# One maximum and one reciprocal for both heads of a pair, in four attention stages of a fused two-block network

## The chip, the cores and the metric

The program runs on one core of a Trainium2 chip. The metric is the device time of one execution in microseconds. Several executions of a kernel are timed; the median stands for it.

## The reference, cut to what matters

The network has two blocks over 512 tokens of width 1024. It holds many matrix products (projections, MLPs, a convolution, a Fourier mixer) and seven kinds of attention, all with 64 wide values and this softmax:

```
s = jnp.where(mask, s.astype(jnp.float32), -jnp.inf)
m = jnp.max(s, axis=-1, keepdims=True)
p = jnp.exp(s - m)
return p / jnp.maximum(jnp.sum(p, axis=-1, keepdims=True), 1e-30)
```

In the neighbourhood attention of the second block a bias is added to the scores of the 256 near keys before the maximum: `s_nb = s_nb + bias[None]`. Everything is float32.

## The kernel before, in words

The program is a list of stages; each of the five engines walks the list and waits on semaphores. Four stages are attention. In each the work is cut into **pairs**: 128 queries (a query tile) of two heads, g = 0 and 1. The pairs of the four stages are:

- the first (from about 226 to 306 us of the profile): 16 causal pairs, in groups of four with 128, 256, 384 and 512 keys, then 16 pairs of a sliding window with 128 or 256 keys and a sink column;
- the second (600 to 755 us): 16 causal pairs as above, whose scores have a second, rotated part, then four rounds of 4 pairs with 31 keys and 8 causal pairs (two groups of four);
- the third (975 to 1175 us): 32 pairs with 768 keys (the "wide" code: the scores of the two heads fill three PSUM banks), then 16 pairs with 256 keys;
- the fourth (2104 to 2232 us): 32 pairs with 512 keys, 256 near ones with the bias and 256 of the context.

The order of work is written out by hand for each engine; `i` counts pairs.

- **TensorE (PE)** at step i: `scores(i)` (lines 1915 to 1939), which first waits until the exponentials of pair i-2 have read the same banks; then `turn(i-2)` (L1953), which transposes the probabilities of pair i-2 into PSUM in up to two "turns", over two banks that alternate; then a part of `weigh` (L1976), the product with the values, for a chunk of two earlier pairs.
- **VectorE (DVE)** at step i: `negmax(i)`, the negated maximum of head 0 and of head 1 (L2918; in the fourth stage each has an addition of the bias ahead, L2914, and waits for it); then `scale(i-1)`, a reciprocal (L2927) and a multiplication of the probabilities (L2933, with gates L2930) for each head; then some copies of turned tiles (L2944) and, after a head pair's last chunk, `take` (L2953, L2957, L2963).
- **ScalarE (ACT)** at step i: the exponential of head 0 and of head 1 (L2335, each followed by a read of its accumulated sum), then the copies of turned tiles of pair i-2 from PSUM (L2347); in the wide stage the copies come first.

The maxima, sums and reciprocals are columns of one small tile. The exponential of head g waited for the maximum of head g alone where a head has at most 512 keys, and for both maxima where it has more:

```
act.wait_ge(negmax_ready, 2 * pair["id"] + 2 if nk > BANK else u + 1)
```

A turn of pair i-2 can start when three things are there: its probabilities are scaled, the bank's last contents have been copied away by ScalarE, and TensorE has come to it.

Of the kernel before, what the change touches and what calls it, by code (L numbers as in the profile page):

```python
# [17 lines left out]
ALU = mybir.AluOpType  # L18
ACT = mybir.ActivationFunctionType
AX = mybir.AxisListType.X  # L20
# [6 lines left out]
ST = S // P  # L27
# [6 lines left out]
BANK = 512  # L34
# [6 lines left out]
ROWS = S // GRID  # L41
# [4 lines left out]
STRIP = 8  # L46
NA_COLS, NA_KEYS = 32, 256
# [217 lines left out]
def build_program(nc, dram, out_dram, stages_kept=10000):  # L265
    ctx = ExitStack()
    with ctx:
# [3 lines left out]
        def sem(name):  # L271
            return ctx.enter_context(nc.semaphore(name))
# [24 lines left out]
        small = sb("small", [P, 64])  # L297
# [7 lines left out]
        psum = ctx.enter_context(nc.psum_tensor("psum", [P, 8 * BANK], F32))  # L305
# [36 lines left out]
        scores_ready, negmax_ready, probs_ready = sem("scores_ready"), sem("negmax_ready"), sem("probs_ready")  # L342
        exp_done, turned = sem("exp_done"), sem("turned")
# [551 lines left out]
        for t in range(4):  # L895
# [6 lines left out]
                gate=lambda qt, g, c=3 * t: GC[:, qt, 12 * g + c:12 * g + c + 1]))  # L902
            for br, (kk, v0) in enumerate(((KS, 0), (KW, 128))):
# [4 lines left out]
                    gate=lambda qt, g, c=3 * t + br + 1: GC[:, qt, 12 * g + c:12 * g + c + 1]))  # L908
# [328 lines left out]
        for t in range(8):  # L1237
# [4 lines left out]
                bias=lambda qt, g, t=t: bias_buf[t % 2][:, g, qt].rearrange("p (r g c) -> p g r c", r=ROWS, c=STRIP),  # L1242
# [766 lines left out]
        def _(act):  # L2009
            steps = [0]  # L2010
            n = dict(tile=0, sq=0, mean=0, unit=0, read=0, scaled=0, idx=0, misc_pe=0, misc_act=0, norm=0, pv=0, normed=0,
                     ctx=0, conv=0, ada=0)
# [288 lines left out]
            def bias_copy(_, i):  # L2301
# [5 lines left out]
                if c == BIAS_STEPS - 1:  # L2307
                    act.wait_ge(bias_copied, i + 1)
                    for h in range(8):
# [7 lines left out]
                        bias=bias_copy, shift=nothing, masked=nothing, compress=compress, compressed=compressed, csquare=context_square,  # L2317
                        csum=context_root, cnorm=context_shift, modrows=lambda *_: copy_rows(), modturn=nothing)

            def attention(st):  # L2320

                pairs = st["pairs"]

                def exponential(pair, i, g):

                    p, nk, off = pair["p"], pair["nk"], pair["off"][g]
                    u = 2 * pair["id"] + g
                    c = u % 8

                    act.wait_ge(negmax_ready, 2 * pair["id"] + 2 if nk > BANK else u + 1)  # L2330
                    if i >= 2:
                        before = [t["seq"] for t in pairs[i - 2]["turns"] if g in t["gs"]]
                        act.wait_ge(turned, before[-1])
                    more = pair["sink"] is not None
                    nc.scalar.activation(pair["probs"][g][:, 0:nk + more], psum[:, off:off + nk + more], ACT.Exp,  # L2335
                                         bias=small[:, c:c + 1], accum_out=small[:, 8 + c:9 + c]).then_inc(exp_done, 1)

                def copies(pair, i):

                    for t in pair["turns"]:  # L2340
                        if t["who"] != "act":
                            continue
                        dst, src = turned_views(pair, t)
                        act.wait_ge(turned, t["seq"])
                        if i >= 4:
                            act.wait_ge(pv_done, st["chunks"][i // 2]["seq"] - 2)
                        nc.scalar.activation(dst, src, ACT.Copy).then_inc(act_copied, 1)  # L2347

                for i in range(len(pairs) + 2):
                    if st["wide"] and i >= 2:  # L2350
                        copies(pairs[i - 2], i - 2)
                    if i < len(pairs):
                        exponential(pairs[i], i, 0)
                        exponential(pairs[i], i, 1)
                    if not st["wide"] and i >= 2:
                        copies(pairs[i - 2], i - 2)
                act.wait_ge(act_copied, pairs[-1]["copied"][0])
# [29 lines left out]
        def _(dve):  # L2387
# [3 lines left out]
            def step(ins):  # L2391
                ins.then_inc(dve_steps, 1)
                steps[0] += 1

            def settle():
                dve.wait_ge(dve_steps, steps[0])

            def chain(ins):

                step(ins)  # L2400
                settle()
# [498 lines left out]
            def attention(st):  # L2900

                pairs, chunks = st["pairs"], st["chunks"]

                def negmax(pair, g):

                    p, nk, off = pair["p"], pair["nk"], pair["off"][g]
                    u = 2 * pair["id"] + g
                    c = u % 8
                    dve.wait_ge(scores_ready, pair["id"] + 1)
                    if p["bias"] is not None:  # L2910
                        if pair["qt"] == 0 and g == 0:
                            dve.wait_ge(bias_in[pair["pi"] % 2], 16 * BIAS_LOADS * (pair["pi"] // 2 + 1))
                        near = psum[:, off:off + NA_KEYS].rearrange("p (g r c) -> p g r c", r=ROWS, c=STRIP)
                        chain(nc.vector.tensor_tensor(near, near, p["bias"](pair["qt"], g), ALU.add))  # L2914
                        if pair["qt"] == ST - 1 and g == 1:
                            dve.sem_inc(bias_used, 1)
                    nk += pair["sink"] is not None
                    nc.vector.tensor_reduce(small[:, c:c + 1], psum[:, off:off + nk], AX, ALU.max,  # L2918
                                            negate=True).then_inc(negmax_ready, 1)

                def scale(pair, g):

                    p, nk = pair["p"], pair["nk"]
                    u = 2 * pair["id"] + g
                    c = u % 8
                    dve.wait_ge(exp_done, u + 1)
                    chain(nc.vector.reciprocal(small[:, 24 + c:25 + c], small[:, 8 + c:9 + c]))  # L2927
                    pb, by = pair["probs"][g][:, 0:nk], small[:, 24 + c:25 + c]
                    if p["gate"] is not None:
                        nc.vector.tensor_scalar(pb, pb, by, p["gate"](pair["qt"], g), ALU.mult,  # L2930
                                                ALU.mult).then_inc(probs_ready, 1)
                    else:
                        nc.vector.tensor_scalar(pb, pb, by, None, ALU.mult).then_inc(probs_ready, 1)  # L2933

                def copies(pair, i):

                    for t in pair["turns"]:
                        if t["who"] != "dve":
                            continue
                        dst, src = turned_views(pair, t)  # L2940
                        dve.wait_ge(turned, t["seq"])
                        if i >= 4:
                            dve.wait_ge(pv_done, chunks[i // 2]["seq"] - 2)
                        nc.vector.tensor_copy(dst, src).then_inc(dve_copied, 1)  # L2944

                def take(chunk):

                    if not chunk["takes"]:
                        return
                    p, c0 = chunk["p"], chunk["c0"]  # L2950
                    dve.wait_ge(pv_done, chunk["seq"])
                    if st["wide"]:
                        nc.vector.tensor_copy(p["dst"][:, c0:c0 + CHUNK], bank(chunk["bank"], CHUNK)).then_inc(o_taken, 1)  # L2953
                        return
                    src = bank(chunk["bank"], p["n"])
                    if p["z"] is not None:
                        nc.vector.tensor_tensor(p["dst"][:, 0:p["n"]], src, p["z"][:, 0:p["n"]],  # L2957
                                                ALU.mult).then_inc(o_taken, 1)
                    else:
                        dst = p["dst"][:, 0:p["n"]]  # L2960
                        if p["runs"] is not None:
                            dst, src = rows_of(dst), by_rows(src)
                        nc.vector.tensor_copy(dst, src).then_inc(o_taken, 1)  # L2963

                for i in range(len(pairs) + 8):
                    if i < len(pairs):
                        negmax(pairs[i], 0)
                        negmax(pairs[i], 1)
                    if 0 <= i - 1 < len(pairs):
                        scale(pairs[i - 1], 0)  # L2970
                        scale(pairs[i - 1], 1)
                    if 0 <= i - 2 < len(pairs):
                        copies(pairs[i - 2], i - 2)
                    j = i - (5 if st["wide"] else 6)
                    if j >= 0 and j % 2 == 0 and j // 2 < len(chunks):
                        take(chunks[j // 2])
                dve.wait_ge(o_taken, chunks[-1]["taken"])
# [244 lines left out]
```

## Time and profile before

| | us |
|---|---|
| median of 3 executions | 3860.42 |
| lowest, highest | 3854.82, 3867.68 |
| span of the profiled execution | 3863.2 |
| TensorE busy | 3731.4 |
| VectorE busy | 1986.4 |
| ScalarE busy | 968.1 |
| GpSimd busy | 585.1 |

The profiled execution is one of its own; the page gives its span and no other time, and its span is 2.8 us above the median. TensorE is busy for 97% of the span, but matmuls are pipelined and "busy" is not "at its peak". In a row of the timeline the first number is the start, the second the duration, and the bracket at the end is how long the engine had been idle and what released it.

### The profile page before, as it was taken

How to read it: one execution, taken by the hardware profiler on the slowest of the kernel's cores; microseconds unless marked ns; L12 is line 12 of the kernel's file. 1: busy time of each engine (PE TensorE's matmuls, PEld its weight loads, DVE VectorE, ACT ScalarE, POOL GpSimd, SP SyncE). 2: the span in 40 equal slices, each digit the busy share in tenths (PEclk: the TensorE clock that was granted, in tenths of full speed). 3: DMA queues.
4: the chain of work that ended last, by engine and by line, in shares of the span. 5: the costliest groups of instructions: out<-in, count | busy, mean ns of one | idle time of the engine just before them, and what ended most of it. 6: DMA issues, size and time to landing. Idle time of an engine off the chain costs nothing.

```text
span 3863.2 us, 42209 instructions
## 1 busy us (share of the span) xinstructions
PE 3731.4 (97%) x16228; PEld 2529.2 (65%) x16232; DVE 1986.4 (51%) x3470; ACT 968.1 (25%) x2234; POOL 585.1 (15%) x476
## 2 busy tenths in 40 slices
PE   9999999999999999999999899999999999999997
PEld 4458445455554655555644588888568888788886
DVE  3654346644773575564301946663765665344343
ACT  2142215521552312112201622021313111221010
POOL 1001000001000111111202411112422111111111
PEclk9999999999999999999999999999999999999998
DMA  3112331022002132333213314543102454122221
GB/s 138 62 43 89 101 106 60 1 93 72 26 1 64 66 122 96 131 109 109 72 67 81 60 44 165 183 153 109 66 22 99 163 175 153 61 73 84 87 85 43
DMA packets 226949, 341.41 MB, mean 88 GB/s; under 512 B 32256, under 2 KB 100512, under 8 KB 226720
## 3 DMA queue, kind: packets, MB, share of 16 engines
q1 hardware_dynamic: 201552, 320.60, 24.2%
q0 software_dynamic: 6816, 10.01, 1.4%
q10 hardware_dynamic: 18384, 8.11, 0.7%
q8 instruction: 132, 2.16, 0.2%
q14 instruction: 65, 0.53, 0.0%
HBM read 333.03 MB, written 4.06 MB: 87 GB/s over the span
## 4 chain that ended last, share of the span: by engine, by line
PE 88%; DVE 6%; ACT 2%; issue 2%; POOL 1%; DMA 1%; ACTq 0%; DVEq 0%; POOLq 0%
PE psum L1856 43%; PE psum L1603 29%; PE psum L1976 3%; PE psum L1923 3%; PE psum L1953 2%; PE psum L1710 1%; DVE small L2918 1%; DVE arena L2591 1%; ACT arena L2347 1%; POOL arena L3106 1%; PE psum L1632 1%; PE psum L1644 1%; PE psum L1661 1%; ACT arena L2335 1%; PE psum L1550 1%
## 5 line engine op out<-in xcount | busy, mean ns | idle before, releaser
L1603 PE MATMUL psum<-HC,ring 128*128 128x256 f32 (+2 forms) x3184 | 1034.1, 484 | 11.7 <-ACT HC L2258 4.5
L1603 PEld LDWEIGHTS psum<-HC,ring 128*128 128x128 f32 (+1 forms) x3184 | 600.1, 190 | 429.2 <-issue 375.2
L1856 PE MATMUL psum<-arena,ring 128*128 128x256 f32 (+1 forms) x2304 | 604.9, 416 | 6.0 <-ACT arena L2110 6.0
L1856 PEld LDWEIGHTS psum<-arena,ring 128*128 128x128 f32 x2304 | 433.6, 190 | 150.3 <-ACT arena L2110 10.9
L1856 PE MATMUL psum<-arena 128*128 128x256 f32 (+1 forms) x1792 | 472.3, 418 | 0.4
L1856 PE MATMUL psum<-HC,ring 128*128 128x256 f32 (+1 forms) x1792 | 435.6, 396 | 4.4 <-ACT arena L2110 4.4
L1856 PEld LDWEIGHTS psum<-arena 128*128 128x128 f32 x1792 | 340.3, 190 | 114.7 <-ACT arena L2115 0.7
L3057 POOL TENSOR_TENSOR ring<-ring 128x1024 f32<-128x1024 f32 (+1 forms) x80 | 217.2, 2715 | 1213.9 <-DVE arena L2415 1183.1
L1856 PEld LDWEIGHTS psum<-HC,ring 128*128 128x128 f32 x1792 | 338.4, 191 | 80.1 <-ACT arena L2110 5.1
L2591 DVE SCALAR_TENSOR_TENSOR arena<-ring,cond,arena 128x512 f32<-128x512 f32 x448 | 318.6, 749 | 8.0
L2484 DVE TENSOR_TENSOR arena<-psum,arena 128x384 f32<-128x384 f32 (+2 forms) x80 | 44.5, 556 | 378.1 <-PE psum L1856 378.0
L2918 DVE TENSOR_REDUCE small<-psum 128x1 f32<-128x512 f32 (+8 forms) x352 | 186.8, 565 | 92.8 <-PE psum L1935 57.8
L2335 ACT ACTIVATE arena<-psum,small 128x256 f32<-128x256 f32 (+8 forms) x320 | 183.4, 577 | 113.7 <-DVE small L2918 78.9
L3030 POOL TENSOR_TENSOR arena<-arena 128x256 f32<-128x256 f32 (+1 forms) x82 | 68.3, 833 | 926.7 <-ACT arena L2236 924.4
L2419 DVE TENSOR_TENSOR arena<-ring,arena 128x1024 f32<-128x1024 f32 (+1 forms) x80 | 201.7, 2521 | 2.7
L1953 PE MATMUL psum<-ident,arena 128*128 128x128 f32 x984 | 150.2, 282 | 34.9 <-ACT arena L2347 23.6
L1856 PE MATMUL psum<-CX,arena 128*128 128x256 f32 x768 | 175.0, 382 | 5.8 <-DVE CX L2438 5.8
L2063 ACT ACTIVATE arena<-psum 128x512 f32<-128x512 f32 (+4 forms) x124 | 58.7, 476 | 457.9 <-PE psum L1603 452.9
L1856 PEld LDWEIGHTS psum<-CX,arena 128*128 128x128 f32 x768 | 146.9, 192 | 27.1 <-issue 6.9
L2110 ACT ACTIVATE arena<-psum 128x384 f32<-128x384 f32 (+2 forms) x80 | 39.1, 489 | 485.5 <-PE psum L1856 485.5
L2347 ACT ACTIVATE arena<-psum 128x512 f32<-128x512 f32 (+3 forms) x272 | 139.7, 552 | 67.7 <-PE psum L1953 67.4
L1953 PEld LDWEIGHTS psum<-ident,arena 128*128 128x128 f32 x984 | 105.9, 142 | 74.5 <-issue 31.8
(236 smaller groups left out, 3834.1 us busy)
## 6 DMA issues: line engine op xcount, KB each, us to landing
ring<-in_mlp_w SPq DMA_DIRECT2D x64, 2048.0 KB, 8.8
ring<-in_ada_w SPq DMA_DIRECT2D x48, 2048.0 KB, 7.9
ring<-in_na_qkv SPq DMA_DIRECT2D x6, 2048.0 KB, 7.9
ring<-in_ab_in SPq DMA_DIRECT2D x5, 2048.0 KB, 9.3
ring<-in_cd_in SPq DMA_DIRECT2D x4, 2048.0 KB, 10.0
ring<-in_pw SPq DMA_DIRECT2D x8, 1024.0 KB, 6.6
ring<-in_at_qkv SPq DMA_DIRECT2D x3, 2048.0 KB, 10.4
ring<-in_ab_out SPq DMA_DIRECT2D x2, 2048.0 KB, 7.8
```

The lines of the kernel that those rows point to most:

```text
L1603: last = nc.tensor.matmul(out, lhs, rhs, start=(k == 0), stop=(k == len(t.pairs) - 1))
L1856: last = nc.tensor.matmul(bank(at, u["T"], u["T"] * m), w[:, i, P * m:P * m + P], x[:, i, :], start=(opens and m == 0 and i == 0), stop=(i ...
L1923: last = nc.tensor.matmul(psum[:, at:at + k1 - k0], p["q"](g, qt * P, qt * P + P), p["k"](g, a * P + k0, a * P + k1), start=(m < 3), stop= ...
L1953: last = nc.tensor.transpose(psum[0:rows, c0:c0 + P], pair["probs"][g][:, k0:k0 + rows], ident[:, :])
L1976: last = nc.tensor.matmul(psum[HD * g:HD * g + HD, at + q0:at + q1], p["v"](g, of[0] if of else kt), chunk["turned"][0:p["krows"], kt, g, ...
L2335: nc.scalar.activation(pair["probs"][g][:, 0:nk + more], psum[:, off:off + nk + more], ACT.Exp, bias=small[:, c:c + 1], accum_out=small[:, ...
L2347: nc.scalar.activation(dst, src, ACT.Copy).then_inc(act_copied, 1)
L2419: nc.vector.tensor_tensor(s4, a12, s2, ALU.subtract).then_inc(s_sums, 1)
L2591: ins = nc.vector.scalar_tensor_tensor(partial[:, v, :], w[:, k, :], cond[:, k, v:v + 1], partial[:, v, :], ALU.mult, ALU.add)
L2918: nc.vector.tensor_reduce(small[:, c:c + 1], psum[:, off:off + nk], AX, ALU.max, negate=True).then_inc(negmax_ready, 1)
L3030: ins = nc.gpsimd.tensor_tensor(total, total, normed.sq[:, k, cols], ALU.add)
L3057: nc.gpsimd.tensor_tensor(a21, a11, a21, ALU.subtract).then_inc(s3_made, 1)
```

## The change

`negmax` and `scale` treat a pair at once. One reduction reads both heads' scores as a view of two groups and writes two columns; one reciprocal takes two columns. In the fourth stage both additions of the bias come ahead of the one reduction, with one wait behind them instead of one behind each. The exponential of either head waits for the pair's reduction; the reciprocal waits for both exponentials. The change is in code that all four attention stages run.

```diff
-                    act.wait_ge(negmax_ready, 2 * pair["id"] + 2 if nk > BANK else u + 1)
+                    act.wait_ge(negmax_ready, pair["id"] + 1)
...
-                        near = psum[:, off:off + NA_KEYS].rearrange("p (g r c) -> p g r c", r=ROWS, c=STRIP)
-                        chain(nc.vector.tensor_tensor(near, near, p["bias"](pair["qt"], g), ALU.add))
...
+                        for g in range(2):
+                            near = psum[:, off[g]:off[g] + NA_KEYS].rearrange("p (g r c) -> p g r c", r=ROWS, c=STRIP)
+                            step(nc.vector.tensor_tensor(near, near, p["bias"](pair["qt"], g), ALU.add))
+                        settle()
...
-                    nc.vector.tensor_reduce(small[:, c:c + 1], psum[:, off:off + nk], AX, ALU.max,
+                    both = psum[:, off[0]:off[0] + 2 * (off[1] - off[0])].rearrange("p (g n) -> p g n", g=2)
+                    nc.vector.tensor_reduce(small[:, c:c + 2], both[:, :, 0:nk], AX, ALU.max,
                                             negate=True).then_inc(negmax_ready, 1)
...
-                    dve.wait_ge(exp_done, u + 1)
-                    chain(nc.vector.reciprocal(small[:, 24 + c:25 + c], small[:, 8 + c:9 + c]))
...
+                    dve.wait_ge(exp_done, u + 2)
+                    chain(nc.vector.reciprocal(small[:, 24 + c:26 + c], small[:, 8 + c:10 + c]))
+                    for g in range(2):
+                        pb, by = pair["probs"][g][:, 0:nk], small[:, 24 + c + g:25 + c + g]
```

On VectorE, in the first stage, around the maxima of the pair with 512 keys (and the scaling of the pair with 384 that follows it), there stood before:

```order
L2918 TENSOR_REDUCE small<-psum 128x1 x2
L2927 RECIPROCAL small<-small 128x1
L2933 TENSOR_SCALAR arena<-arena,small 128x384
L2927 RECIPROCAL small<-small 128x1
L2933 TENSOR_SCALAR arena<-arena,small 128x384
```

and there stands now:

```order
L2920 TENSOR_REDUCE small<-psum 128x2 [waits scores_ready]
L2929 RECIPROCAL small<-small 128x2 [waits exp_done]
L2936 TENSOR_SCALAR arena<-arena,small 128x384 [waits dve_steps]
L2936 TENSOR_SCALAR arena<-arena,small 128x384
```

Six engine instructions have become four, and the maxima of both heads arrive together. On VectorE in the fourth stage, one pair's step was this, with the semaphores that each row waits for:

```order
L2914 TENSOR_TENSOR psum<-psum,CX 128x256 [waits bias_in0,scores_ready]
L2918 TENSOR_REDUCE small<-psum 128x1 [waits dve_steps]
L2914 TENSOR_TENSOR psum<-psum,CX 128x256 [waits scores_ready]
L2918 TENSOR_REDUCE small<-psum 128x1 [waits dve_steps]
L2927 RECIPROCAL small<-small 128x1 [waits exp_done]
L2933 TENSOR_SCALAR sd_rstd<-sd_rstd,small 128x512 [waits dve_steps]
L2927 RECIPROCAL small<-small 128x1 [waits exp_done]
L2933 TENSOR_SCALAR sd_rstd<-sd_rstd,small 128x512 [waits dve_steps]
```

and is this now:

```order
L2914 TENSOR_TENSOR psum<-psum,HC 128x256 [waits bias_in1,scores_ready]
L2914 TENSOR_TENSOR psum<-psum,HC 128x256
L2920 TENSOR_REDUCE small<-psum 128x2 [waits dve_steps]
L2929 RECIPROCAL small<-small 128x2 [waits exp_done]
L2936 TENSOR_SCALAR sd_rstd<-sd_rstd,small 128x512 [waits dve_steps]
L2936 TENSOR_SCALAR sd_rstd<-sd_rstd,small 128x512
```

The addition for head 1 has moved ahead of the only reduction. The order on ScalarE and TensorE is the same as before.

## Rows read from the trace of the kernel before

**Rows 1.** The page: the chain that ended last, by engine

```profile
PE 88%; DVE 6%; ACT 2%; issue 2%; POOL 1%; DMA 1%; ACTq 0%; DVEq 0%; POOLq 0%
```

**Rows 2.** Busy time by engine in the four attention stages (window and length first)

```profile
226.00:306.00 80.00, 74.88 (x622) 46.89 (x624) 56.70 (x200) 52.45 (x171) 0.00 (x0) 1.00 0.08 28
600.00:755.00 155.00, 143.79 (x1071) 80.38 (x1070) 109.25 (x393) 101.81 (x351) 0.00 (x0) 0.99 0.04 15
975.00:1175.00 200.00, 181.93 (x1210) 112.91 (x1212) 155.02 (x342) 120.23 (x274) 0.00 (x0) 1.00 0.05 13
2104.00:2232.00 128.00, 103.16 (x869) 71.58 (x870) 107.54 (x263) 83.17 (x195) 62.88 (x112) 0.96 0.40 75
```

**Rows 3.** Timeline, first stage: maxima, exponentials, copies, TensorE

```profile
237.60 0.76 DVE L2918 TENSOR_REDUCE small<-psum 128x1 f32<-128x256 f32 x2 [1.16 <-PE psum L1935]
...
239.01 1.08 ACT L2347 ACTIVATE arena<-psum 128x512 f32<-128x512 f32 x2
...
240.12 1.02 DVE L2918 TENSOR_REDUCE small<-psum 128x1 f32<-128x384 f32 x2 [0.98 <-PE psum L1935]
...
240.23 1.08 PE L1976 MATMUL psum<-arena 128*64 128x256 f32 x8
...
242.95 1.29 DVE L2918 TENSOR_REDUCE small<-psum 128x1 f32<-128x512 f32 x2 [0.89 <-PE psum L1935]
...
243.68 0.69 ACT L2335 ACTIVATE arena<-psum,small 128x512 f32<-128x512 f32 x1 [1.46 <-DVE small L2918]
...
245.02 0.59 ACT L2347 ACTIVATE arena<-psum 128x512 f32<-128x512 f32 x1
...
245.75 0.41 PE L1953 MATMUL psum<-ident,arena 128*128 128x128 f32 x2 [0.39 <-ACT arena L2347]
```

**Rows 4.** Timeline, second stage: a pair with 512 keys in a later round

```profile
687.46 0.69 ACT L2335 ACTIVATE arena<-psum,small 128x512 f32<-128x512 f32 x1 [0.75 <-PE psum L1953]
```

**Rows 5.** Timeline, third stage: a pair with 768 keys

```profile
1021.45 1.82 DVE L2918 TENSOR_REDUCE small<-psum 128x1 f32<-128x768 f32 x2 [1.39 <-PE psum L1923]
1022.03 1.08 ACT L2347 ACTIVATE arena<-psum 128x512 f32<-128x512 f32 x2 [3.22 <-PE psum L1953]
...
1022.78 0.41 PE L1953 MATMUL psum<-ident,arena 128*128 128x128 f32 x2 [0.34 <-ACT arena L2347]
```

**Rows 6.** Timeline, third stage: its pairs with 256 keys

```profile
1152.26 0.76 DVE L2918 TENSOR_REDUCE small<-psum 128x1 f32<-128x256 f32 x2 [0.21 <-PE psum L1923]
...
1153.38 0.16 DVE L2927 RECIPROCAL small<-small 128x1 f32<-128x1 f32 x1
...
1153.99 0.44 PE L1953 MATMUL psum<-ident,arena 128*128 128x128 f32 x2 [0.56 <-DVE arena L2933]
```

**Rows 7.** Timeline, fourth stage: VectorE's part of one pair's step

```profile
2163.60 0.42 DVE L2914 TENSOR_TENSOR psum<-psum,HC 128x256 f32<-128x256 f32 x1
2164.06 0.69 DVE L2918 TENSOR_REDUCE small<-psum 128x1 f32<-128x512 f32 x1
...
2166.97 0.43 DVE L2914 TENSOR_TENSOR psum<-psum,HC 128x256 f32<-128x256 f32 x1
```

**Rows 8.** Timeline, fourth stage: ScalarE and TensorE around the same step

```profile
2160.98 1.30 PE L1976 MATMUL psum<-arena 128*64 128x128 f32 x12
...
2162.21 1.14 PE L1915 MATMUL psum<-arena 64*128 64x256 f32 x8
...
2165.85 0.69 ACT L2335 ACTIVATE arena<-psum,small 128x512 f32<-128x512 f32 x1 [0.29 <-DVE small L2918]
...
2166.52 1.07 ACT L2347 ACTIVATE arena<-psum 128x512 f32<-128x512 f32 x2
...
2167.26 1.11 PE L1953 MATMUL psum<-ident,sd_rstd 128*128 128x128 f32 x8 [0.33 <-ACT arena L2347]
```

**Rows 9.** The chain that ended last, fourth stage: two pieces four pairs apart

```profile
2152.81 1.11 PE psum L1953 x8
...
2167.26 0.79 PE psum L1953 x5
```

More of the change, by code:

```diff
@@ L2902, in attention, with negmax @@
                 pairs, chunks = st["pairs"], st["chunks"]
[L2904 to L2908, printed above, removed]
+                def negmax(pair):
+                    p, nk, off = pair["p"], pair["nk"], pair["off"]
+                    c = 2 * pair["id"] % 8
                     dve.wait_ge(scores_ready, pair["id"] + 1)
                     if p["bias"] is not None:
-                        if pair["qt"] == 0 and g == 0:
+                        if pair["qt"] == 0:
@@ L2912, in negmax @@
                             dve.wait_ge(bias_in[pair["pi"] % 2], 16 * BIAS_LOADS * (pair["pi"] // 2 + 1))
-                        near = psum[:, off:off + NA_KEYS].rearrange("p (g r c) -> p g r c", r=ROWS, c=STRIP)
-                        chain(nc.vector.tensor_tensor(near, near, p["bias"](pair["qt"], g), ALU.add))
-                        if pair["qt"] == ST - 1 and g == 1:
+                        for g in range(2):
+                            near = psum[:, off[g]:off[g] + NA_KEYS].rearrange("p (g r c) -> p g r c", r=ROWS, c=STRIP)
+                            step(nc.vector.tensor_tensor(near, near, p["bias"](pair["qt"], g), ALU.add))
@@ L2916, in negmax, with scale @@
+                        settle()
+                        if pair["qt"] == ST - 1:
                             dve.sem_inc(bias_used, 1)
                     nk += pair["sink"] is not None
-                    nc.vector.tensor_reduce(small[:, c:c + 1], psum[:, off:off + nk], AX, ALU.max,
+                    both = psum[:, off[0]:off[0] + 2 * (off[1] - off[0])].rearrange("p (g n) -> p g n", g=2)
+                    nc.vector.tensor_reduce(small[:, c:c + 2], both[:, :, 0:nk], AX, ALU.max,
                                             negate=True).then_inc(negmax_ready, 1)
-                def scale(pair, g):
+                def scale(pair):
@@ L2923, in scale @@
                     p, nk = pair["p"], pair["nk"]
-                    u = 2 * pair["id"] + g
+                    u = 2 * pair["id"]
                     c = u % 8
-                    dve.wait_ge(exp_done, u + 1)
-                    chain(nc.vector.reciprocal(small[:, 24 + c:25 + c], small[:, 8 + c:9 + c]))
[L2928 to L2933, printed above, removed]
+                    dve.wait_ge(exp_done, u + 2)
@@ new lines, in scale @@
+                    chain(nc.vector.reciprocal(small[:, 24 + c:26 + c], small[:, 8 + c:10 + c]))
+                    for g in range(2):
+                        pb, by = pair["probs"][g][:, 0:nk], small[:, 24 + c + g:25 + c + g]
+                        if p["gate"] is not None:
+                            nc.vector.tensor_scalar(pb, pb, by, p["gate"](pair["qt"], g), ALU.mult,
+                                                    ALU.mult).then_inc(probs_ready, 1)
+                        else:
+                            nc.vector.tensor_scalar(pb, pb, by, None, ALU.mult).then_inc(probs_ready, 1)
@@ L2966, in attention @@
                     if i < len(pairs):
-                        negmax(pairs[i], 0)
-                        negmax(pairs[i], 1)
+                        negmax(pairs[i])
                     if 0 <= i - 1 < len(pairs):
-                        scale(pairs[i - 1], 0)
-                        scale(pairs[i - 1], 1)
+                        scale(pairs[i - 1])
                     if 0 <= i - 2 < len(pairs):
```

## The prediction

> **What bounds the kernel now.** The chain that ended last is 88% TensorE and 6% VectorE [rows 1]: work taken off VectorE counts only where TensorE stands still for it. So I read the four attention stages, the only ones that the change reaches. Their busy times [rows 2] say that TensorE works 74.88 of 80 us, 143.79 of 155, 181.93 of 200 and 103.16 of 128; VectorE is at 71%, 70%, 78% and 84%. TensorE's gaps are 5 + 11 + 18 + 25 = 59 us in all, and only these can move. [...] Then I read the timeline of each stage for what ends TensorE's gaps.
>
> First stage [rows 3]: TensorE ends the scores of the 512-key pair at 242.9; VectorE begins its two maxima at 242.95; the exponential of head 0 starts at 243.68, as soon as the first maximum is there, after ScalarE stood idle for 1.46; both exponentials take until 245.02, where the copies start; 0.73 behind that, at 245.75, TensorE resumes turning after a gap of 0.39 that the bracket puts down to the copy. The chain is first maximum, exponential, exponential, copy, turn. The second maximum (0.6 us) runs beside the first exponential and costs nothing.
>
> In the third stage the exponential waited for both maxima already where there are 768 keys, and TensorE's gap of 0.34 ends on a copy that had waited 3.22 us for TensorE itself [rows 5]: VectorE has no part in it. In its pairs with 256 keys the gap of 0.56 ends on VectorE's second multiplication [rows 6].
>
> In the fourth stage VectorE runs back to back: one pair's step starts at 2163.60 and the next at 2166.97 [rows 7]. TensorE's turn at 2167.26 waits for a copy behind the second exponential, which starts at 2165.85, when the second maximum is there [rows 8]. Four pairs take 2167.26 - 2152.81 = 14.45 us [rows 9].
>
> **The price of the merged instructions.** Two reductions together take 0.76, 1.02, 1.29 and 1.82 us for 256, 384, 512 and 768 keys per head [rows 3, 5]: 1.035 ns an element and 0.23 fixed. One alone over 512 takes 0.69 [rows 7], so 0.16 is fixed in one. One over 2x512 should take 0.16 + 1.06 = 1.22: the merge saves 0.07 and delays the *first* maximum from 0.69 to 1.22, by 0.53. For 384 keys the delay is 0.40, for 256 it is 0.26. No row shows a reduction with two groups. Its bounds are 1.15 (another 0.07 saved) and 1.38 (the two groups cost two full instructions); I take 1.22, since the line through the rows is straight. The second reciprocal goes, with its wait: from its start to the next multiplication 0.2 us (1153.38 to about 1153.6, the first row's duration plus a wait) [rows 6]. A reciprocal of two columns is taken as the 0.16 of one; at most it is twice that.
>
> **Part by part.**
>
> 1. *512-key pairs of the causal groups.* Four in the first stage, four in the second's first part and four in the last group of its four rounds: 12 pairs whose chain is that of rows 3. The first exponential is 0.53 later, and TensorE has no other work in that gap: 12 x 0.53 = **+6.4**. Everything that ScalarE has queued behind (second exponential, copies, the next pair's exponential) moves along.
> 2. *Pairs with 256 keys behind a 512-key pair.* ScalarE's copies at 239.01 last until 240.09, and TensorE's weighing at 240.23 begins 0.14 after, exactly the copy's latency [rows 3]. The pair's first exponential comes up to 0.26 later, the copies with it; I take 0.2, with 7 such places (three in the first stage, four in the rounds; in the rotated scores of the second stage TensorE has more to do first): **+1.4**. For the 384-key pairs the copies end well before they are wanted: nothing.
> 3. *The other 512-key pair of each round.* Its first exponential waits for TensorE (0.75), which waited for VectorE's scaling of earlier pairs [rows 4]. VectorE gains 0.07 + 0.2 in each of three pairs ahead, 0.8 in all, but the merged maximum of the pair itself then ends last: I take 0.35 earlier, between 0 and 0.8: 4 x -0.35 = **-1.4**.
> 4. *Pairs with 768 keys*: **0**. VectorE's shorter step only waits longer for scores.
> 5. *Pairs with 256 keys of the third stage.* The chain scores, maxima, scaling, turn loses 0.07 and 0.2 once in two pairs, less than the gap of 0.56: 8 x -0.25 = **-2.0**. A doubled price of the two-column reciprocal would leave -0.8.
> 6. *Fourth stage.* Let N be the start of a pair's first addition. Before, TensorE's turn came at N + 3.66 (2163.60 to 2167.26) [rows 7, 8]. Now: addition 0.33 (0.42 less the 0.09 by which consecutive instructions overlap, as 2 x 0.69 against 1.29 shows), addition and wait 0.46, reduction 1.22, so the maxima are there at N + 2.01 instead of about N + 2.2 for head 1, but instead of N + 1.15 for head 0; exponentials from N + 2.04, 0.67 each (243.68 to 245.02 for two) [rows 3]; copies at N + 3.38; the turn 0.74 later (2166.52 to 2167.26) [rows 8], at N + 4.12. From a turn, TensorE needs 1.05 for it (1.11 less the overlap), 1.23 for weighing, 1.14 for the scores of two pairs on (2160.98, 2162.21) [rows 8], and 0.02: the next N of the same parity is 3.44 after the turn. The loop over two pairs is 3.44 + 4.12 = 7.56, four pairs take 15.12 instead of 14.45. VectorE's own step shrinks from 3.37 by 0.20 in the maxima and 0.20 in the reciprocals to 2.97, and is no longer in the loop. Of the stage's eight fours I leave out the first, which starts up: 7 x 0.67 = **+4.7**. If two additions without a wait between need 0.46, it is 1.8 more.
>
> Sum: 6.4 + 1.4 - 1.4 - 2.0 + 4.7 = +9.1. Against the profiled execution that is 3863.2 + 9.1 = 3872.3; its span is 2.8 above the median, so the median is forecast at **3869.5**. Merged reductions at their bounds move the 12 pairs and the 14 steps of the loop, 26 x -0.07 = -1.8 or 26 x 0.16 = +4.2; with the reciprocal, the additions and point 3, the likeliest case spans +5 to +17.
>
> [...]
>
> **The rivals.**
>
> *A: VectorE's time decides the fourth stage (faster).* VectorE is back to back there [rows 7], and each step loses 0.40: 1.6 per four pairs, to 12.85. (TensorE's own work would be 4 x 3.42 = 13.7 if every weighing took the 1.23 of rows 8; some are shorter, so I let VectorE's figure stand.) 7 x -1.6 = -11.2; with points 3 and 5 and no delay elsewhere the time is 3860.4 - 14.6 = **3846**. For it: back-to-back rows and 84%. Against it: the turn's bracket names ScalarE's copy, and two exponentials that overlapped the second maximum now come after both. It decides if copies are ready less than 0.5 later than I work out. With the 7.8 of points 1 and 2 kept, it ends at 3854. [...]
>
> *B: every delay of head 0 reaches TensorE (slower).* Then the 256- and 384-key pairs of the 12 causal groups pay 0.26 + 0.40 each: 12 x 0.66 = 7.9 in place of 1.4, +15.6 in all, **3876**. For it: their maxima too start only when TensorE's scores end (gaps of 1.16 and 0.98 ahead of them), so the exponentials have no lead [rows 3]. Against: TensorE weighs at 240.23, while the 384-key maxima of 240.12 are still being taken, with work of older pairs [rows 3].
>
> *C: nothing reaches the end.* The gap of 0.39 at 245.75 would be filled from work that is ready, and gains and losses cancel: **3860**. TensorE's order is fixed, so only a gain ahead of it can do this.
>
> **How the numbers follow.** The likeliest case (+5 to +14 around 9) has 0.50, B 0.20, C 0.15, A 0.15. 0.3%, 11.6 us, is about what a measurement of this kernel can tell from no change. The likeliest case leaves 0.36 within it and 0.14 above; B lies above but for 0.03; C is within; A splits, 0.09 below (faster), 0.06 within. With a little of the executions' own spread: faster 0.10, same 0.55, slower 0.35. The range for 8 in 10 is 3853 to 3880; it leaves out A's full gain and the far end of B.
>
> **What would show it.** VectorE's busy time falls by about 176 x (0.07 + 0.15) = 39 us, whatever happens to the end. Right: a merged reduction of 1.2 us for 2x512; the exponential behind it at the scores' end + 1.3; TensorE's gap in rows 3 at 0.9 instead of 0.39; four pairs of the fourth stage at 15.1; the gap in rows 6 at 0.3. Wrong: a reduction of 1.4 or more, four pairs at 13 to 14 (rival A), or gaps in front of the weighing and scores of 256- and 384-key pairs (B).

## The result, and the profile after

The changed kernel takes 3877.95 us (median of 5, 3872.26 to 3888.0) against 3860.42 (3854.82 to 3867.68): the ratio is 1.0047, with a 95% interval of 1.0034 to 1.006. The change makes the kernel slower by 13 to 23 us. The time lies in the stated range, near its upper end; the time that was called likeliest, 3869.5, is 8.5 us too low, and "slower by over 0.3%" had been given 0.35.

The page of the changed kernel: its span, busy time by engine, and the chain that ended last by engine.

```profile
span 3870.4 us, 41857 instructions
...
PE 3729.6 (96%) x16228; PEld 2527.4 (65%) x16232; DVE 1949.4 (50%) x3118; ACT 964.2 (25%) x2234; POOL 585.1 (15%) x476
...
PE 89%; DVE 4%; ACT 3%; issue 2%; POOL 1%; DMA 1%; ACTq 0%; DVEq 0%; POOLq 0%
```

VectorE's busy time fell by 37 us (39 were forecast), and the program got longer. Against [rows 1], VectorE's share of the chain fell from 6% to 4% and ScalarE's rose from 2% to 3%. The profiled execution is the fastest of the five (3872.26 us with what lies around its span), so whole spans of the two profiles are not to be subtracted; the steps inside them are.

The timeline of the changed kernel in the first stage, at the place of [rows 3]:

```profile
242.14 1.23 DVE L2920 TENSOR_REDUCE small<-psum 128x2 f32<-128x1024 f32 x1 [1.29 <-PE psum L1935]
...
243.40 0.69 ACT L2335 ACTIVATE arena<-psum,small 128x512 f32<-128x512 f32 x1 [1.73 <-DVE small L2920]
...
244.74 0.59 ACT L2347 ACTIVATE arena<-psum 128x512 f32<-128x512 f32 x1
...
245.48 0.30 PE L1953 MATMUL psum<-ident,arena 128*128 128x128 f32 x1 [0.98 <-ACT arena L2347]
```

The reader is to follow one chain down the four rows. The merged maximum takes 1.23 us; the exponential starts 1.26 after the reduction's start, where it started 0.73 after it; the copy comes 1.34 later, the turn 0.74 after that. TensorE's gap is 0.98 instead of 0.39.

The fourth stage, at the place of [rows 7, 8], and then the chain's turns, two pairs apart, to be held against [rows 9]:

```profile
2164.62 0.76 DVE L2914 TENSOR_TENSOR psum<-psum,HC 128x256 f32<-128x256 f32 x2 [1.38 <-PE psum L1915]
2165.42 1.23 DVE L2920 TENSOR_REDUCE small<-psum 128x2 f32<-128x1024 f32 x1
2166.68 0.69 ACT L2335 ACTIVATE arena<-psum,small 128x512 f32<-128x512 f32 x1 [1.97 <-DVE small L2920]
...
2168.02 1.08 ACT L2347 ACTIVATE arena<-psum 128x512 f32<-128x512 f32 x2
...
2168.76 1.11 PE L1953 MATMUL psum<-ident,sd_rstd 128*128 128x128 f32 x8 [1.29 <-ACT arena L2347]
```

```profile
2161.16 1.11 PE psum L1953 x8
...
2168.76 1.11 PE psum L1953 x8
...
2176.35 1.12 PE psum L1953 x8
```

VectorE, which had been back to back, now stands idle for 1.38 us ahead of its additions. From the first addition to the turn it is 2168.76 - 2164.62 = 4.14 us (4.12 worked out, 3.66 before); two pairs take 7.60, four 15.19 (15.12 worked out, 14.45 before). In the kernels e5, e6 and e8 below, which merge nothing in this stage, four pairs take 14.36; by that measure the change costs 0.83 in four pairs rather than 0.74.

The third stage's pairs with 256 keys are the place where the change gains: TensorE's gap is 0.30 (0.56 in [rows 6]), and two pairs take 3.82 instead of 4.08.

```profile
1160.36 0.69 DVE L2920 TENSOR_REDUCE small<-psum 128x2 f32<-128x512 f32 x1 [0.21 <-PE psum L1923]
...
1161.84 0.33 PE L1953 MATMUL psum<-ident,arena 128*128 128x128 f32 x1 [0.30 <-DVE arena L2936]
```

So each step of the prediction is there, but their sum does not reach the measured loss. A kind of loss that the sum has no term for shows in the second stage. This is TensorE's timeline of the changed kernel there:

```profile
716.82 0.55 PE L1953 MATMUL psum<-ident,arena 128*128 128x128 f32 x3
718.29 0.87 PE L1953 MATMUL psum<-ident,arena 128*128 128x128 f32 x3 [0.93 <-ACT arena L2347]
```

and the busy times of two stretches around it (length, the engines, then the granted clock as the third number from the right):

```profile
713.00:717.00 4.00, 3.75 (x26) 1.80 (x25) 3.77 (x8) 2.81 (x11) 0.00 (x0) 1.00 0.00 0
717.00:722.00 5.00, 4.08 (x21) 2.13 (x21) 1.92 (x6) 2.71 (x9) 0.00 (x0) 0.66 0.00 0
```

The same three transposes take 0.55 us before a gap of 0.93 and 0.87 behind it: in slices of 0.25 us the granted clock is 1.00 up to 718.00, 0.50 from 718.25 to 721.50 and 1.00 again from 721.75. The two maxima at 717.07 and 721.73 lie 4.66 apart, where the same two are 3.21 apart a round earlier: 1.45 us lost on top of the gap. The prediction has no term for this.

Such a fall is not new. The kernel before has one at the same place of an earlier round, behind a gap of 0.50 (in slices of 0.5 us the granted clock is 0.50 from 662.50 to 665.50 and 1.00 from 666.00), and its two maxima there are 4.05 apart instead of 2.60:

```profile
661.50 0.55 PE L1953 MATMUL psum<-ident,arena 128*128 128x128 f32 x3
662.56 0.87 PE L1953 MATMUL psum<-ident,arena 128*128 128x128 f32 x3 [0.50 <-ACT arena L2347]
```

And the same gap of 0.93, a round earlier in the changed kernel (692.12), has no fall behind it: the granted clock is 1.00 from 690 to 697. The two profiles alone can't say whether the change brings more of them: both executions have a mean clock of 0.991. The other four executions of the changed kernel have 0.987 to 0.989, so it takes means over many executions.

### The profile page after: what moved, and what is told of

It reads as the page before. It is cut to its first block, busy times and chain, and to the rows that moved or that the text cites. A ratio compares the mean times of both kernels' runs of the same rounds, so it can differ in the third digit from the quotient of the medians.

```text
span 3870.4 us, 41857 instructions
## 1 busy us (share of the span) xinstructions
PE 3729.6 (96%) x16228; PEld 2527.4 (65%) x16232; DVE 1949.4 (50%) x3118; ACT 964.2 (25%) x2234; POOL 585.1 (15%) x476
## 4 chain that ended last, share of the span: by engine, by line
PE 89%; DVE 4%; ACT 3%; issue 2%; POOL 1%; DMA 1%; ACTq 0%; DVEq 0%; POOLq 0%
PE psum L1856 43%; PE psum L1603 29%; PE psum L1976 3%; PE psum L1923 3%; PE psum L1953 3%; PE psum L1710 1%; DVE small L2920 1%; DVE arena L2591 1%; ACT arena L2347 1%; ACT arena L2335 1%; POOL arena L3107 1%; PE psum L1632 1%; PE psum L1644 1%; PE psum L1661 1%; PE psum L1550 1%
## 5 line engine op out<-in xcount | busy, mean ns | idle before, releaser
L2920 DVE TENSOR_REDUCE small<-psum 128x2 f32<-128x1024 f32 (+8 forms) x176 | 172.6, 981 | 121.5 <-PE psum L1935 78.3
```

The source lines that it names most:

```text
L2920: nc.vector.tensor_reduce(small[:, c:c + 2], both[:, :, 0:nk], AX, ALU.max, negate=True).then_inc(negmax_ready, 1)
```

## How time at full clock and time lost to the clock are told apart

Each run comes with its span and its mean granted clock. Span x clock is taken as the length that the run would have had at a granted clock of 1.00 throughout (called full clock below), and span x (1 - clock) as what the clock took, as far as TensorE is what the program waits for. That this holds well here is seen in the changed kernel alone: its five runs have spans of 3870.4, 3875.0, 3886.1, 3876.1 and 3877.6 us at clocks of 0.991, 0.989, 0.987, 0.989 and 0.989; 0.004 of clock goes with 15.7 us, and 0.004 of the span is 15.5. And four sets of 14 to 28 runs of the kernel before, on different occasions, have means of span x clock of 3824.5, 3824.4, 3825.0 and 3824.8. The clock is printed to 0.001, 3.9 us, so only means over runs are used; I take them to be good to about 1 us, as an estimate. The last column and the one on span x clock are means over the runs of a kernel against the kernel before in the same set. Of the executions of the kernel before that were timed beside the changed kernel no clock is on record; there, 3824.5 and the clocks of the other sets are used.

| kernel | runs | ratio (95%) | span x clock, less before | forecast of that | mean clock (before) |
|---|---|---|---|---|---|
| the change | 5 | 1.0047 (1.0034 to 1.006) | +9.9 | +9.1 | 0.9890 (0.9911 to 0.9915) |
| e1_wait_both | 5 | 1.0078 (1.0064 to 1.0091) | +15.5 | +18 | 0.9876 (0.9915) |
| e2_recip_only | 11 | 0.9999 (0.999 to 1.0008) | -5.0 | -4.5 | 0.9901 (0.9915) |
| e3_max_only | 5 | 1.0062 (1.0049 to 1.0074) | +13.0 | +14 to +17 | 0.9886 (0.9915) |
| e4_fourth_only | 11 | 1.0021 (1.0012 to 1.003) | +5.3 | +4.7 | 0.9908 (0.9915) |
| e5_third_only | 11 | 0.9995 (0.9986 to 1.0004) | -2.9 | -2 | 0.9910 (0.9911) |
| e6_first_two_only | 6 | 1.003 (1.0019 to 1.0042) | +6.1 | +6.5 | 0.9897 (0.9911) |
| e7_mixed | 11 | 0.999 (0.9981 to 0.9999) | -6.6 | -6 | 0.9903 (0.9911) |
| e8_wait_short | 11 | 1.001 (1.0001 to 1.0019) | +2.2 | +2 | 0.9907 (0.9911) |
| e9_wait_512 | 5 | 1.0051 (1.0037 to 1.0065) | +6.0 | +8 | 0.9874 (0.9911) |
| e10_late_two | 11 | 0.9995 (0.9986 to 1.0003) | -5.1 | -5 | 0.9904 (0.9911) |
| e11_split_512 | 11 | 1.0004 (0.9995 to 1.0013) | +2.4 | +3 to +4 | 0.9913 (0.9911) |

## The experiments

All were made from one source in which each of the four attention stages chooses for itself whether a pair has one reduction, one reciprocal, the additions of the bias ahead, and whether an exponential waits for both maxima. With no stage chosen it does what the kernel before does, but for a wait on the scores once a pair instead of once a head; with all chosen it is the changed kernel. It was not run with no stage chosen. Its fourth stage, where left as it was, takes 14.36 us for four pairs and not 14.45 (see above), some 0.6 us in the stage.

```diff
+                    one = stage_no in MERGED_MAX
+                    attn["maxed"] += 1 if one else 2
+                    m = attn["maxed"]
+                    pair.update(one_max=one, one_recip=stage_no in MERGED_RECIP, hoisted=one or stage_no in HOISTED,
+                                maxed=[m, m] if one or split or stage_no in BOTH_WAIT else [m - 1, m])
...
-                    act.wait_ge(negmax_ready, 2 * pair["id"] + 2 if nk > BANK else u + 1)
+                    act.wait_ge(negmax_ready, pair["maxed"][g])
```

### Nothing merged, only the wait (e1)

```diff
+MERGED_MAX, MERGED_RECIP, HOISTED, BOTH_WAIT = (), (), (), (1, 2, 3, 4)
```

> The kernel before, with nothing merged: two maxima and two reciprocals a pair as before, but either exponential waits for the maxima of both heads in all four stages. If the loss comes from head 0's exponential starting late, it costs more than the change did, since the second maximum now ends 0.6 us behind the first instead of 0.53: the first stage's four pairs take 10.25 + 0.6 + 0.3 = 11.1 us, the fourth stage's 15.5 instead of 14.45, and all together +18 us (12 x 0.60, 7 x 0.27, 4 x 0.4, 7 x 1.07). If the loss came from the merged instructions themselves, this is within 3 us of the kernel before.

It is 25 to 35 us slower. Four pairs of the first stage take 11.06 us, two of the fourth 7.80 (15.6 for four). The wait of head 0's exponential alone costs more than the whole change; the merged instructions are not what loses. At full clock it is +15.5 where +18 was expected; what makes it 2.5 less is not shown. Its mean clock is 0.9876 against 0.9915, which takes as much again.

### One part of the change alone (e2, e3)

```diff
+MERGED_MAX, MERGED_RECIP, HOISTED, BOTH_WAIT = (), (1, 2, 3, 4), (), ()
...
+MERGED_MAX, MERGED_RECIP, HOISTED, BOTH_WAIT = (1, 2, 3, 4), (), (1, 2, 3, 4), ()
```

> The kernel before with only the reciprocals merged (one of two columns, waiting for both exponentials). Theory of the late exponential: no loss anywhere, -0.2 us for each two pairs with 256 keys of the third stage (3.88 instead of 4.08), fourth stage 14.2 instead of 14.45 per four pairs, rounds of the second stage 0 to 0.4 shorter; -4.5 us in all, same to faster. Rival, that waiting for both exponentials costs: the third stage's last part or the fourth stage gets longer, slower by some us.

Two pairs of the fourth stage take 7.125 us (14.25 for four). At full clock the kernel gains 5.0, as expected; but its mean clock is 0.9901 against 0.9915, which takes 5 back, and the time is that of the kernel before.

> The change without the merged reciprocal: one reduction a pair, additions of the bias ahead of it, two reciprocals. Theory of the late exponential: the whole loss and a little more, since the gain of the reciprocal is missing: 10.92 per four pairs of the first stage as in the changed kernel, 15.1 in the fourth, 4.02 per two pairs in the last part of the third; +14 to +17 us. Rival, that the reciprocal costs: less than half of the loss stays.

10.93 us for four pairs of the first stage, 7.59 for two of the fourth; +13.0 at full clock, a little under the forecast, and a clock of 0.9886. The whole loss comes with the merged reduction (and, in the fourth stage, the additions ahead of it); the merged reciprocal hides 3 us of it.

### Stage by stage (e4, e5, e6)

```diff
+MERGED_MAX, MERGED_RECIP, HOISTED, BOTH_WAIT = (4,), (4,), (4,), ()
...
+MERGED_MAX, MERGED_RECIP, HOISTED, BOTH_WAIT = (3,), (3,), (), ()
...
+MERGED_MAX, MERGED_RECIP, HOISTED, BOTH_WAIT = (1, 2), (1, 2), (), ()
```

> The whole change, in the fourth stage alone. Working of the loop: four pairs take 15.1 us instead of 14.45, +4.7 in the stage. Rival (VectorE's time decides that stage): four pairs take 12.9 to 13.7, -5 to -11 us. Whether the time beyond the stages' own lengths (the granted clock) goes with it shows in the whole: +5 if not, up to +9 if so.

Two pairs take 7.60 us. Rival A is out: VectorE was saved some 0.40 in every step of a stage in which it had next to no idle time, and the stage got longer. The kernel is +5.3 at full clock, and its clock of 0.9908 against 0.9915 takes some 3 us more.

> The whole change, in the third stage alone. By the working of the prediction nothing for 768 keys and -0.25 us for each two pairs with 256 keys, 3.83 instead of 4.08: -2 us in the stage. Mean clock as before if the clock goes with gaps: 3857 us. If the time beyond the stages' own lengths was noise of that program and not the clock, no statement.

The stage from its first to its last maximum is 191.37 us long instead of 193.25. No change in the time that can be told from none.

> The whole change, in the first two stages alone, the complement of the two kernels with the fourth and the third. Late exponential: first stage +2.4, second +4 from their own steps at full clock. If the rest of the loss is TensorE's clock, which falls in more or longer gaps, the mean granted clock falls too (0.990 instead of 0.9915) and the whole is +10 to +14; if the clock has no part, +6.5.

+6.1 at full clock, and a clock of 0.9897 against 0.9911: here is most of the loss of clock. The three kernels' parts at full clock, 5.3 - 2.9 + 6.1 = 8.5, are the change's 9.9 within the means' error.

### Which pairs bring the clock down (e8, e9, e11)

```diff
-                                maxed=[m, m] if one or split or stage_no in BOTH_WAIT else [m - 1, m])
+                                maxed=[m, m] if one or split or (stage_no < 3 and 256 <= nk < 512) else [m - 1, m])
...
-                                maxed=[m, m] if one or split or stage_no in BOTH_WAIT else [m - 1, m])
+                                maxed=[m, m] if one or split or (stage_no < 3 and nk == 512) else [m - 1, m])
...
-                    one = stage_no in MERGED_MAX
+                    one = stage_no in MERGED_MAX and not (stage_no < 3 and nk == 512)
```

> The kernel before, with the exponentials waiting for both maxima only in the pairs with 256 to 384 keys (257 in the sliding window) of the first two stages. Working of the prediction: only the 256-key pairs behind a 512-key pair pay, 10.25 becomes 10.5 in the first stage, 11.56 stays in the second, 25.5 becomes 25.8 in a round; +2 us at full clock. Rival B (every delay of head 0 reaches TensorE): four pairs take 10.9 and 12.2, +8 us at full clock.

Four pairs take 10.45 us in the first stage (10.25 before), 11.56 in the second (11.56), and a round 25.79 (25.5). Rival B is out, though its sum of 3876 was the nearest to the measured time: the delay of head 0 in these pairs reaches TensorE at one place in a group of four, behind a 512-key pair, and not in every pair.

> The kernel before, with the exponentials waiting for both maxima only in the 512-key pairs of the first two stages (16 pairs). Working of the prediction: 10.25 becomes 10.85 for four pairs of the first stage, 11.56 becomes 12.16 in the second, 25.5 becomes 26.5 in a round; +8 us at full clock. The clock: this kernel makes the long gaps of TensorE (0.4 to 1.0) that the wait in the 256- and 384-key pairs alone did not make. If long gaps bring the clock down, the mean clock is 0.990 or less and the time +13 to +16; if the clock has another cause (the merged instructions), it stays at 0.991 and the time at +8.

Four pairs take 10.85 in the first stage and 12.16 in the second's first part, to the hundredth as worked out. At full clock it is +6.0, the time is +14 to +25, and the difference is the clock, 0.9874 against 0.9911. The second stage's rounds are where it goes. Busy times of that stage in three kernels, first e9_wait_512:

```profile
600.00:773.00 173.00, 155.82 (x1087) 88.64 (x1085) 109.60 (x394) 102.42 (x353) 0.00 (x0) 0.92 0.04 13
```

then e8_wait_short:

```profile
600.00:755.00 155.00, 143.33 (x1073) 80.34 (x1073) 109.18 (x392) 101.98 (x351) 0.00 (x0) 1.00 0.04 15
```

and e11_split_512:

```profile
600.00:753.00 153.00, 143.60 (x1074) 80.66 (x1074) 96.34 (x276) 101.83 (x351) 0.00 (x0) 1.00 0.04 15
```

The kernel with the long gaps ran this stage at a mean of 0.92, so the clock took, by this estimate, 0.08 x 173 = 14 us of it; the others lost nothing to it here, and [rows 2] has 0.99 for the kernel before. From its first to its last pair of maxima the stage takes 157.8 us in e9_wait_512, 143.4 in e8_wait_short and 141.1 in e11_split_512. One of the falls in e9_wait_512, in TensorE's timeline and in two stretches around it:

```profile
723.54 0.55 PE L1961 MATMUL psum<-ident,arena 128*128 128x128 f32 x3
725.01 0.88 PE L1961 MATMUL psum<-ident,arena 128*128 128x128 f32 x3 [0.93 <-ACT arena L2355]
```

```profile
720.00:724.50 4.50, 3.76 (x25) 1.75 (x23) 4.36 (x15) 3.08 (x10) 0.00 (x0) 1.00 0.00 0
724.50:730.00 5.50, 4.99 (x21) 3.00 (x21) 2.67 (x10) 2.49 (x9) 0.00 (x0) 0.51 0.00 0
```

It has the same place in a round as the falls at 718.29 in the changed kernel and at 662.56 in the kernel before: the turn of the 384-key pair. What the moved wait adds is the length of the gap, 0.93 instead of 0.50. The number of falls goes with it: read in slices of 1 us from 600 to 775, the clock falls to 0.50 six times in e9_wait_512, once in the kernel before and not at all in e8_wait_short and e11_split_512.

> The changed kernel with one thing undone: the 16 pairs with 512 keys of the first two stages have two reductions and single waits again, everything else is merged. This takes the long gaps away and nothing else. At full clock 12 x 0.53 = 6.4 us less than the changed kernel, which leaves +3 to +4. If those gaps are also what brought the clock down, the mean clock rises from 0.989 to 0.990 or more and the time is +4 to +9 instead of +17.5; if not, the clock stays at 0.989 and the time is +11 to +13.

This is the other side of it. With two reductions again in 16 of 176 pairs, and everything else merged, the clock is back at 0.9913 and the time is within 0.13% of the kernel before. The timeline of e11_split_512 at the place of [rows 3]:

```profile
242.15 1.29 DVE L2940 TENSOR_REDUCE small<-psum 128x1 f32<-128x512 f32 x2 [1.29 <-PE psum L1943]
...
244.95 0.52 PE L1961 MATMUL psum<-ident,arena 128*128 128x128 f32 x3 [0.39 <-ACT arena L2355]
```

The gap is 0.39 again. Of the change's 17.5 us these 16 pairs carry some 14 to 15: 7.5 at full clock, and the clock's share. That is a comparison across two sets of executions, each against the kernel before.

### What gains, alone (e7, e10)

```diff
+MERGED_MAX, MERGED_RECIP, HOISTED, BOTH_WAIT = (3,), (1, 2, 3, 4), (4,), ()
...
+MERGED_MAX, MERGED_RECIP, HOISTED, BOTH_WAIT = (3,), (3, 4), (4,), ()
```

> Only what should gain: one reciprocal in all stages, one reduction only in the third stage (where the exponentials waited for both anyway), both additions of the bias ahead in the fourth stage but two reductions. Steps at full clock: third stage 3.83 for two pairs, fourth stage 14.1 for four, -6 us in all. If the clock pays it back as it did with the merged reciprocal alone (0.990 against 0.9915), the time is that of the kernel before; if it does not, 3853.

Two pairs of the fourth stage take 7.07 us (14.13 for four). 6.6 us less at full clock, and 3857.34 against 3859.84 in the median: 0.1% faster, at the edge of what can be told. It is the only version whose interval lies wholly under that of no change, and by little.

> What gains, without the two stages in which the merged reciprocal went with a lower clock: one reduction only in the third stage, one reciprocal in the third and the fourth, both additions ahead in the fourth. At full clock -2 to -3 in the third stage and -2.7 in the fourth. If the clock stays at 0.991, -5 us, 3854 to 3855; if it pays back here too, the time of the kernel before.

-5.1 at full clock, but a clock of 0.9904 against 0.9911, and no difference that can be told. The guess that the clock falls only where the first two stages' reciprocals are merged was wrong.

## Why the prediction was half right

- **What bounds the kernel**: right. In the first two stages the chain of the 512-key pair ran through the first maximum, and ScalarE's copy released TensorE; e1 shows it by moving only the wait.
- **The merged instructions' price**: right. 1.23 us for 2x512 (1.22 taken), 0.69 for 2x256, 0.96 for 2x384; a second group costs nothing that can be seen, as 0.69 is also the time of one group of 512. The reciprocal of two columns takes 0.15 to 0.17, as one column does. Two additions without a wait take 0.76 together, a pitch of 0.33.
- **Point 1** (+6.4): right, in the second stage's first part to the hundredth: 12.16 for 11.56 in e9, with a delay of 0.60, and 12.09 to 12.10 in the changed kernel, with 0.53.
- **Point 2** (+1.4): right. Four pairs of the first stage take 10.92, +0.67, of which 0.53 is point 1 and 0.14 this (0.2 taken); e8 shows the place alone.
- **Point 3** (-1.4): wrong in size. A round takes 26.17 us (673.11 to 699.28) instead of 25.5, so +0.67, where 0.53 of point 1, 0.2 of point 2 and -0.35 of this one give +0.38. With 512-key pairs unmerged (e11) it takes 25.2, so the gain of 0.3 is there; but merging the maxima of both 512-key pairs of a round costs 0.97 and not 0.53. The step "the merged maximum of the pair itself then ends last" was seen, and its price was set too low: it takes back all of the gain.
- **Points 4 and 5** (0 and -2.0): right, 3.82 for two pairs, and e5 has -1.9 us in the stage.
- **Point 6** (+4.7): right, 7.60 for a loop worked out at 7.56; e4 has +5.3. The 14.45 that it starts from is 14.36 in the kernels made from the common source, which is 0.6 of the difference.
- **The sum**: right as a sum at full clock, +9.1 against +9.9. **The step that failed** is the one from there to the time: the sum has no term for the granted clock, as if the change left it alone. The runs show that it does not: the mean clock fell from some 0.9913 to 0.9890, which is 8 to 10 us, as much as all the waits together. Nor was the clock at 1.00 before the change: the 0.96 over 128 us in [rows 2] comes to 5 us by span x (1 - clock), in two falls to 0.50 (2109 to 2114 and 2126 to 2134, the second beginning inside a gap of 7.36 us that ends at 2129.36).
- **The range**: the measured time lies in it by luck in part. The upper end of 3880 reaches up for rival B's 3876, and rival B is refuted; the likeliest case alone (the prediction gives it once as +5 to +17 and once as +5 to +14) ends at about 3877 or 3874.
- **The rivals**: A was wrong (e4), B was wrong (e8) with a number that came near the measured time; no rival had the mechanism that was missing. The granted clock of 0.96 and 0.99 in two of the four stages [rows 2] was a hint that it does fall in them.

What stays open is when the clock falls. That the mean clock comes down with the longer gaps of the 512-key pairs is shown by e9 against e8 (0.9874 and 0.9907) and by e11 against the change. But no run tells why the gap of 0.93 at 718.29 has a fall behind it and the one at 692.12 has none. And in e2, e7 and e10 the clock is lower as well (0.9901, 0.9903 and 0.9904 against 0.9915, 0.9911 and 0.9911), though no gap of TensorE is longer in the first three stages of their profiles. In the fourth, from 2170 to 2220 us, the longest gap of a step is 0.82 in e2 and 0.76 in e7 and e10, against 0.76 in e8, where the stage is as before; in e11 it is 1.29, and e11, which also has the merged reciprocal in all stages, has a clock of 0.9913. So neither these gaps nor the merged reciprocal explain it by themselves. Some 3 to 5 us of gain are lost to that.

## What to carry to other kernels

Merging two instructions on an engine that had time to spare made the first result wait for the second (the exponential came 1.26 us after the reduction's start instead of 0.73): ask who takes the first result, and whether its chain is what TensorE waits for. An engine that is back to back need not be the bound either: here the fourth stage lost 0.7 to 0.8 us in four pairs although VectorE was saved some 1.6. And with gaps of 0.93 instead of 0.50 us in the second stage's rounds (e9) the mean granted clock was 0.9874 instead of 0.9911, which is 14 us: the forecast needed a second term for TensorE's clock. Read the granted clock by stretch and compare the means of span x clock between kernels, which repeated to 0.6 us over four sets here, while the mean spans differed by 2.1.

## What the runs showed of the hardware that was not expected

A reduction over two groups, 2x512, in one VectorE instruction takes 1.23 us, where two instructions took 1.29: only 0.06 to 0.07 us is saved by a merge, as consecutive instructions overlap by 0.09 (2 x 0.69 less 1.29). And in two places the granted clock fell within a gap of 0.93 us on TensorE: from 1.00 to a mean of 0.51 over 5.5 us, after a stretch in which TensorE worked 3.76 of 4.50 us (e9), and to a mean of 0.66 over 5 us, after 3.75 of 4.00 (the changed kernel). Such a gap did not always go with a fall, nor was it needed: the gap of 0.98 in the changed kernel's first stage left the clock at 1.00 (243 to 250 us), and in the kernel before a gap of 0.50 had the fall of 662.5 at its end.
